# Building the expert gates: one-hot rows moved from GpSimd to VectorE and ScalarE

## The reference

```
i1 = jnp.take_along_axis(si[:, :, 0], ci // P_TOPK, axis=-1)
i2 = jnp.take_along_axis(si[:, :, 1], ci % P_TOPK, axis=-1)
experts = (i1 * P_N_KEYS + i2).reshape(t, P_HEADS * P_TOPK)
gates = jax.nn.softmax(best, axis=-1).reshape(t, P_HEADS * P_TOPK)
...
a = jnp.einsum('td,tkd->tk', hb, u_tab[eb])
w = gb.astype(hb.dtype) * jax.nn.gelu(a, approximate=False)
return jnp.einsum('tk,tkd->td', w, v_tab[eb])
```

## Time and profile before

| | |
|---|---|
| time, median of 2 runs | 4259.78 us (4255.82 to 4263.74) |
| profiled execution | 4253.08 us, of it span 4251.2 us |
| PE busy over the span | 3881.9 us (91%) |
| DVE busy | 3525.9 us (83%) |
| ACT busy | 1930.8 us (45%) |
| POOL busy | 1112.7 us (26%) |
| copies of gate matrices to `g_buf` | 192, the first starts at 947.9 us, the last at 3262.4 us |
| one-hot instructions | 672 + 192 on DVE, 288 on POOL, 96 on ACT |

### The profile page before, as it was taken

One profiled execution on the slowest core, in us unless ns is written; L12 is line 12 of the kernel. 1 busy time (PEld: TensorE's weight loads), 2 busy tenths in 40 slices (PEclk: granted clock), 3 DMA queues, 4 the chain that ended last, 5 costly groups with the idle time before them and its releaser, 6 DMA issues. The chain is left out here.

```text
span 4251.2 us, 69821 instructions
## 1 busy us (share of the span) xinstructions
PE 3881.9 (91%) x23631; PEld 3349.5 (79%) x23631; DVE 3525.9 (83%) x6891; ACT 1930.8 (45%) x3591; POOL 1112.7 (26%) x1095
## 2 busy tenths in 40 slices
PE   7968899988899999999999888898967999999998
PEld 6854468887788888888888876445856999999998
DVE  5387857999799999999999965665998999999998
ACT  4356523137544444444444355553246544444443
POOL 0000000019544334444343300000037333333332
PEclk9979999959999999999999988999969999999999
DMA  5102221137899999999999911112227999999997
GB/s 192 44 28 64 70 80 40 61 105 197 288 373 377 372 375 380 377 378 375 374 375 375 350 60 51 39 45 75 75 80 236 374 374 372 372 372 370 377 369 290
DMA packets 246964, 1018.18 MB, mean 240 GB/s; under 512 B 17088, under 2 KB 115488, under 8 KB 146608
## 3 DMA queue, kind: packets, MB, share of 16 engines
q0 software_dynamic: 85296, 599.59, 36.4%
q1 hardware_dynamic: 161472, 416.31, 27.8%
HBM read 963.34 MB, written 52.43 MB: 239 GB/s over the span
## 5 line engine op out<-in xcount | busy, mean ns | idle before, releaser
L1374 POOL DMA_INDIRECT rows<-rows,pick_i x512 | 797.4, 1557 | 1156.4 <-DVE y_tok L2629 643.8
L522 PE MATMUL psA<-h_hi,split_hi 128*128 128x448 f32 (+3 forms) x2768 | 968.7, 350 | 97.8 <-DVE xT L2608 50.7
L2006 DVE TENSOR_TENSOR split_lo<-raw,split_hi 128x1024 fp32r<-128x1024 f32 x596 | 727.3, 1220 | 322.8 <-ACT split_hi L1417 316.2
L522 PE MATMUL psA<-h_lo,split_hi 128*128 128x448 f32 (+3 forms) x2768 | 948.9, 343 | 0.0
L522 PE MATMUL psA<-h_hi,split_lo 128*128 128x448 f32 (+3 forms) x2768 | 948.5, 343 | 0.0
L1417 ACT ACTIVATE split_hi<-raw 128x1024 fp32r<-128x1024 f32 x596 | 628.5, 1054 | 327.8 <-DMA raw<-expert_pairs 150.9
L522 PEld LDWEIGHTS psA<-h_hi,split_hi 128*128 128x128 f32 x2768 | 525.5, 190 | 174.2 <-issue 121.3
L2617 DVE CUSTOM_DVE_ANT_1 rows<-rows,h_wide 128x1024 f32<-128x1024 f32 x512 | 624.1, 1219 | 10.9 <-DMA rows<-rows,pick_i 8.6
L2629 DVE SCALAR_TENSOR_TENSOR y_tok<-rows,pick_w,y_tok 128x1024 f32<-128x1024 f32 x444 | 568.6, 1281 | 5.9
L522 PEld LDWEIGHTS psA<-h_hi,split_lo 128*128 128x128 f32 x2768 | 525.2, 190 | 35.5
L522 PEld LDWEIGHTS psA<-h_lo,split_hi 128*128 128x128 f32 x2768 | 526.1, 190 | 33.1
(11 more groups left out here) (340 smaller groups left out, 6319.9 us busy)
## 6 DMA issues: line engine op xcount, KB each, us to landing
raw<-expert_pairs SPq DMA_DIRECT2D x256, 1024.0 KB, 7.2
gates<-g_buf SPq DMA_DIRECT2D x24, 2048.0 KB, 8.7
raw<-tiles SPq DMA_DIRECT2D x84, 512.0 KB, 3.7
raw<-mod_tiles SPq DMA_DIRECT2D x80, 512.0 KB, 3.6
g_in<-gates POOLq DMA_DIRECT2D x32, 896.0 KB, 9.0
g_in<-gates POOLq DMA_DIRECT2D x32, 640.0 KB, 5.8
mod_w<-mod_pairs SPq DMA_DIRECT2D x8, 1024.0 KB, 19.9
rows<-rows,pick_i POOLq DMA_INDIRECT x512, 8.5
```

The costliest lines, as they stand in the source:

```text
L522: ins = nc.tensor.matmul(out_, lhsT, rhs, start=start, stop=stop)
L1374: nc.gpsimd.indirect_dma_start(rows[l][:, b, :], None, (rows0, rows1)[l], bass.IndirectOffsetOnAxis(pick_i[:, u:u + 1], 0))\
L2006: V.tensor_tensor(split_lo[:, n % SPLIT].rearrange("p k n -> p (k n)"), raw[:, n % RAW, :], split_hi[:, n % SPLIT].rearrange("p k n -> p ( ...
```

## The change

GpSimd's part of the gate stage goes, with its semaphores and the tile `first_key`. VectorE makes all four first-key rows of each group in one instruction of 512 elements per partition, and three weighted rows in each group. ScalarE makes the fourth weighted row of every group, not of every odd one: before the loop for the groups 0, 1 and 2, then in each group for the one three further on. TensorE waits for `oh_last` and `oh_ready` in every group.

```diff
@@ TensorE, build_gates
-                seen.enter(i, {oh_ready: 2 * GROUPS, oh_first: 2 * GROUPS, oh_last: GROUPS, psum_A_free: 2 * GROUPS})
+                seen.enter(i, {oh_ready: 2 * GROUPS, oh_last: 2 * GROUPS, psum_A_free: 2 * GROUPS})
                 for g in range(2 * GROUPS):
-                    pe.wait_ge(oh_first, seen.upto(oh_first))
-                    if g % 2:
-                        pe.wait_ge(oh_last, seen.upto(oh_last))
+                    pe.wait_ge(oh_last, seen.upto(oh_last))
                     pe.wait_ge(oh_ready, seen.upto(oh_ready))
@@ GpSimd
-            pool.wait_ge(sel_copied, seen.upto(sel_copied, NTT - DENSE[l][0] // P))
...
-                    pool.wait_ge(oh_passed, seen.at(oh_passed, base + g - 2 + (2 * GROUPS * steps if last else 0)))
...
-                        nc.gpsimd.tensor_copy(first_key[:, (g + 1) % 4], idxT[:, 0, bass.ds(t, 2)]).then_inc(pool_chain, 1)
...
-                    for j in range(g % 2, 2):
-                        ins = nc.gpsimd.tensor_scalar(onehot[:, g % 4, 0, 2 + j], iota, first_key[:, g % 4, j:j + 1], None,
-                                                      ALU.is_equal)
-                    ins.then_inc(oh_first, 1)
...
@@ ScalarE, build_gates
                     for g in range(b * GROUPS, (b + 1) * GROUPS):
-                        helps = g % 2 == 0 and g < count
+                        helps = g < count
                         t = i * (2 * TB) + (start + 4 * (g + ahead) + 3)
                         if helps:
                             key_distance(t)
@@
-            key_distance(start + 4 + 3)
-            last_one_hot(1, start + 4 + 3)
+            for g in range(ahead):
+                key_distance(start + 4 * g + 3)
+                last_one_hot(g, start + 4 * g + 3)
             with act.Fori(0, rounds - 1) as i:
-                seen.enter(i, {psum_A_full: 2 * GROUPS, psum_A_free: 2 * GROUPS, oh_distance: GROUPS, oh_last: GROUPS,
+                seen.enter(i, {psum_A_full: 2 * GROUPS, psum_A_free: 2 * GROUPS, oh_distance: 2 * GROUPS, oh_last: 2 * GROUPS,
@@ VectorE, build_gates
-                    n = 2 + g % 2
-                    V.tensor_tensor(onehot[:, g % 4, 0, 0:n], iota.unsqueeze(1).broadcast_to([P, n, P]),
-                                    idxT[:, 0, bass.ds(t, n)].unsqueeze(2).broadcast_to([P, n, P]), ALU.is_equal)
-                    for j in range(4 - g % 2):
+                    V.tensor_tensor(onehot[:, g % 4, 0], iota.unsqueeze(1).broadcast_to([P, 4, P]),
+                                    idxT[:, 0, bass.ds(t, 4)].unsqueeze(2).broadcast_to([P, 4, P]), ALU.is_equal)
+                    for j in range(3):
                         ins = V.tensor_scalar(onehot[:, g % 4, 1, j], iota, idxT[:, 1, bass.ds(t + j, 1)],
                                               idxT[:, 2, bass.ds(t + j, 1)], ALU.is_equal, ALU.mult)
                     ins.then_inc(oh_ready, 1)
```

More of the change, by code:

```diff
@@ L186, in build_program @@
     act_chain = semaphore("act_chain")
-    pool_chain = semaphore("pool_chain")
     dve_chain = semaphore("dve_chain")
@@ L265, in build_program @@
     oh_ready = semaphore("oh_ready")
-    oh_first = semaphore("oh_first")
     oh_last = semaphore("oh_last")
@@ L301, in build_program @@
     small = place("small", [P, 160])
-    first_key = place("first_key", [P, 4, 2])
     ident2 = place("ident2", [P, HALF])
@@ L1331, in _ @@
             tb0, tb1 = gate_blocks(l)
-            pool.wait_ge(sel_copied, seen.upto(sel_copied, NTT - DENSE[l][0] // P))
[L1333 to L1339, removed]
-                    pool.wait_ge(oh_passed, seen.at(oh_passed, base + g - 2 + (2 * GROUPS * steps if last else 0)))
-                    pool.wait_ge(pool_chain, seen.upto(pool_chain))
-                    if not last:
-                        t = i * (2 * TB) + (tb0 * TB + 4 * (g + 1) + 2)
-                        nc.gpsimd.tensor_copy(first_key[:, (g + 1) % 4], idxT[:, 0, bass.ds(t, 2)]).then_inc(pool_chain, 1)
-                    elif g < 2 * GROUPS - 1:
-                        t = (tb1 - 2) * TB + 4 * (g + 1) + 2
-                        nc.gpsimd.tensor_copy(first_key[:, (g + 1) % 4], idxT[:, 0, t:t + 2]).then_inc(pool_chain, 1)
-                    for j in range(g % 2, 2):
-                        ins = nc.gpsimd.tensor_scalar(onehot[:, g % 4, 0, 2 + j], iota, first_key[:, g % 4, j:j + 1], None,
-                                                      ALU.is_equal)
-                    ins.then_inc(oh_first, 1)
[L1354 to L1358, removed]
             for b in range(2):
```

## The result

| | before | after |
|---|---|---|
| time, median | 4259.78 us | 4320.76 us (4320.15 to 4321.37) |
| ratio | 1 | 1.016, 95% interval 1.014 to 1.0181 |
| profiled execution | 4253.08 us | 4320.15 us |
| its span | 4251.2 us | 4318.3 us |
| gate stage of layer 0, first copy's start to last copy's end | 150.1 us | 191.7 us |

The two gate stages grew by 41.6 and 27.6 us, together 69.2 us; the span grew by 67.1. Nothing else in the kernel moved by more than a microsecond or so: the first copy came 0.7 us earlier, the stretch between the stages shrank by 0.9 and the one behind them by 0.5.

What follows compares the result with a forecast made beforehand. VectorE was taken to bound the gate stage at 1.36 us a group, ScalarE afterwards at 1.77. Terms +65.6, +2.6, -3.6 and -0.6 gave +64 us on 4253.08, plus 6.7 for the median: 4324 us, range 4302 to 4352.

Steps and rivals of the forecast that it cites:

- What bounded the stage before: Gate stage before the change: VectorE sets the pace at 1.36 us a group, with GpSimd just behind.
- VectorE's new group: Gate stage, VectorE with four first-key and three weighted rows: 1.39 us a group, or 1.33 if weighted rows get faster.
- ScalarE's period: Gate-stage loop: distance, copy and one-hot take 0.31 + 0.83 + 0.63 = 1.77 us a group, bounds 1.66 and 1.94.
- The sum: Both gate stages: +65.6 inside loops, +2.6 and -3.6 behind them, -0.6 at the start, together +64 us.
- the 26 helping groups: Behind the loops, 13 groups per layer where ScalarE still makes a one-hot: 1.46 us each, +2.6 us in all.
- the last three of each layer: Last three groups per layer, needing no ScalarE one-hot as their rows are made: 2 x -1.8 = -3.6 us.
- the -0.6 at the start: Start of each layer's gate stage: TensorE no longer waits for GpSimd, 0.3 us a layer.
- Rival A, ACT fits in: Gate stage: ScalarE's gaps shrink and its period falls under VectorE's 1.39 us; -6 to +6 us, chance 0.05.
- Rival B, ACT slower still: Gate stage: one-hot to distance takes 0.80 us or waits are added, period from 1.90 us; 4345 to 4360 us, chance 0.12.
- Rival C, PE's clock: Gate stage: TensorE, less busy, drops to 1.2 GHz and added waits make it the pace; 4347 us, chance 0.05.

Runs made afterwards that it cites:

- balanced version: Kernel before with one GpSimd and three VectorE first-key rows per group, ScalarE's fourth weighted row every group, distance a group ahead, copy wait per block: 4235.1 us, 0.9963.
- ScalarE pipelined: Changed kernel with ScalarE's distance made one group ahead into one of two tiles and its copy wait only at block ends: 4255.84 us, 1.0004 of before.

## Why the prediction was right, point by point

- **What bounded the stage before.** VectorE, at 1.36 us a group. Moving ScalarE's wait there changed nothing; the gain of the balanced version came with a lighter VectorE group; and TensorE's groups began 0.24 us after VectorE's last row. The mean over the loops is 1.345 us, a little less than the pair of groups that the prediction read.
- **VectorE's new group.** 1.39 us expected, 1.37 measured where it runs free (ScalarE pipelined). The first-key row cost 0.14 us as read from the two forms (0.61 us from the four-row instruction to the next). The weighted rows came out at 0.255 us without GpSimd. The group lies nearer the upper bound (1.39) than the lower (1.33), which took 0.02 us a row off the odd group, whose rows already stepped by 0.26. It did not matter, as this engine was no longer the pace.
- **ScalarE's period.** 1.77 expected, 1.76 measured, of 0.31, 0.82 and 0.63 against 0.31, 0.83 and 0.63. The one step that the trace of before did not have, one-hot to distance, was rightly taken from the copy to distance step with the same kind of wait and one address. Behind the loop the period is 1.44 to 1.45 us against 1.46. ScalarE's busy share was forecast as 84% and came out as 22.92 / 30 = 76%. The forecast divided the sum of the durations by the period, but the profile's busy time counts overlapping instructions once (the section on the profile before calls it a sum of durations, which it is not), and the copy lasts 577 ns here (median) where 597 was taken. This touched no term of the sum.
- **The sum.** +64 expected, +69.2 in the stages of the profile. Inside the loops the copies of before took 215.2 us for 160 groups and those of after 285.2, so +70.0 where 65.6 was expected. Behind the loops the 26 helping groups gave +1.9 (2.6 expected) and the last three of each layer -2.7 (-3.6); the -0.6 at the start lies ahead of the stage as measured here. Of the 4.4 us missed inside the loops, 2.4 come from the pace of before, 160 x (1.36 - 1.345). The rest is at the ends of the loop's rounds: the step from the one-hot to the distance there is 1.10 us and not 0.63,

```profile
1002.99 0.49 ACT L1840 ACTIVATE onehot<-distance,idxT,minus_gate 128x128 f32<-128x128 f32 x1 [0.24 <-ACT g_buf L1857]
1004.09 0.40 ACT L1835 ACTIVATE distance<-cst,idxT 128x128 f32<-128x128 f32 x1 [0.61 <-ACT onehot L1840]
```

  a gap of 0.61 us, eight times in the two layers, 8 x 0.47 = 3.8 us, of which the period of 1.76 in place of 1.77 gives back 1.6. At the entry of the loop the prediction had read a step of 0.80 and had used it as the upper bound of every group, not as a cost of the loop's edge by itself. Half rounds, where a block ends, show 0.22 instead of 0.14, as forecast. The runs' medians differ by 61.0 us and the forecast was 64 for those, so the time was missed by 3.2 us, 4324 against 4320.76. That this is less than the miss in the stages, and on the other side, is luck: the two runs of before have a median of 4259.78, while 14 to 19 runs of the same kernel beside the experiments gave 4254.2 to 4254.7.
- **Rival A, ACT fits in.** It needed the 0.25 and the 0.14 gap to go. They did not, in the changed kernel. The overlap that the Trainium skill states ("ScalarE: Activation LUTs", section "What ACT_TABLE_LOAD costs") is there where the engine does not wait for what it has just issued: 0.10 us from one-hot to distance with ScalarE pipelined (0.39 us start to start, 0.49 long). It is not there in this kernel's two other steps.
- **Rival B, ACT slower still.** Only at the round ends.
- **Rival C, PE's clock.** The clock did fall, for some 3 us at a time, but it decided nothing; see the last section.

## What to carry to other kernels

An engine that waits for its own instructions has a period that its busy share doesn't show: at 76% busy ScalarE set the pace here, and added work on a VectorE at 81% was free. Before moving work to an engine with idle time, add up start-to-start steps of the sequence that it will repeat, with the gaps behind its own semaphores, and compare that period with the pace. Where it is too long, first move the waits off the sequence (one more tile, a wait at the end of a block): in this kernel this gave back 66 of the 69 us that the change cost (326.2 to 259.9 us in the stages), where moving the rows alone won nothing.

## What the runs showed of the hardware

**GpSimd and VectorE disturb each other.** Without GpSimd every weighted row of VectorE steps by 0.256 us. Beside a busy GpSimd most still do, but one or two in a group step by 0.27 to 0.31: 0.28 on the mean in the even group shown before, 0.27 in the balanced version. A GpSimd one-hot of the same size took 650 ns (median) where VectorE was busy 21 of 30 us, 708 where it was busy all the time, and 1176 in the balanced version, where nearly each of them overlaps with VectorE's instruction that reads two tiles, 0.55 us long. The Trainium skill, "GPSIMD Engine Reference", section "1. Specifications", says that GpSimd's SBUF interfaces are shared with VectorE, and names contention with VectorE instructions in a two-port mode or with two inputs in SBUF. The trace agrees for the latter: 1176 ns is 0.53 us more than the 644 of those that met no such instruction. VectorE's instruction itself stayed at 0.55 us.

**A lower TensorE clock that costs nothing.** In the changed kernel, with PE busy 20.92 of 30 us, the clock fell twice inside layer 0's stage, at 978 and at 1092 us. Windows of 2 us, columns as in the earlier trace rows:

```profile
978.00:980.00 2.00, 1.40 (x10) 1.21 (x9) 1.46 (x4) 1.52 (x4) 0.00 (x0) 0.83 1.01 290
980.00:982.00 2.00, 2.00 (x10) 1.74 (x10) 1.46 (x4) 1.48 (x4) 0.00 (x0) 0.50 1.01 291
982.00:984.00 2.00, 1.77 (x12) 1.58 (x11) 1.86 (x5) 1.62 (x4) 0.00 (x0) 0.81 0.67 192
```

From 980 to 982 us the granted clock is 0.50 (1.2 GHz) and PE is busy all of the 2.00 us; then it comes back. ScalarE's distances start at 979.01, 980.77 and 982.53, still 1.76 us apart:

```profile
979.01 0.40 ACT L1835 ACTIVATE distance<-cst,idxT 128x128 f32<-128x128 f32 x1
...
980.77 0.40 ACT L1835 ACTIVATE distance<-cst,idxT 128x128 f32<-128x128 f32 x1
...
982.53 0.40 ACT L1835 ACTIVATE distance<-cst,idxT 128x128 f32<-128x128 f32 x1
```

Two copies that each waited for TensorE at the lower level were 1.64 us apart before, under the 1.76 of this stage, so PE kept up. What PE did before the fall, and at the next end of a loop's round, where the clock stayed at 1.00:

```profile
977.25 1.15 PE L519 MATMUL psA<-onehot 128*128 128x128 f32 x8 [1.08 <-ACT onehot L1840]
...
1005.84 1.15 PE L519 MATMUL psA<-onehot 128*128 128x128 f32 x8 [1.07 <-ACT onehot L1840]
```

PE stood idle for 0.60 us ahead of each group and for 1.08 at the end of a round. The Trainium skill ("TensorE: Matmul & The Clock Gate", section "A second HAM failure mode: psum-queue depth-cycling") says that short idle spells between groups make the clock swing. These rows agree in part. The rounds of the two layers end in eight such longer spells; the clock fell after three of them (977, 1092 and 3283 us) and stayed at 1.00 after the other five, as here at 1005.84. Before, with PE busy 85%, it stood at 1.00. What tells the three from the five no run here shows.

**The untouched rest of the kernel varies more than the effect.** Between the end of layer 0's gate stage and the start of layer 1's, where no edit reaches, the profiled runs took from 2053.8 to 2066.5 us. Medians of a few runs don't settle 8 us here; the stage's own length in the trace does.
